# HGRN decays on one Trainium2 core: decayed keys from ScalarE's exponential, queries multiplied on GpSimd

## The reference, cut to what matters

```python
logf = logaddexp(log(lb), log1p(-lb) + log_sigmoid(f_logit))
k = -expm1(logf)
bc = cumsum(logf)                      # within a chunk, per feature
decay = exp(bc[t] - bc[s])             # for s <= t
scores = einsum(q[t], k[s], decay)
o = scores @ v
```

## Time and profile before

| what | value |
|---|---|
| median of 3 runs | 1686.91 us (1686.0 to 1687.82) |
| the profiled execution's own time | 1685.33 us |
| its span in the profile | 1683.5 us |
| mean granted TensorE clock | 0.995 of full |
| layer 0's HGRN levels (first and last score matmul) | 122.05 to 167 us |
| the same in layer 1 | 476.42 to 521 us |

### The profile page before, as it was taken

One profiled execution on the slowest core, in us unless ns is written; L12 is line 12 of the kernel. 1 busy time (PEld: TensorE's weight loads), 2 busy tenths in 40 slices (PEclk: granted clock), 3 DMA queues, 4 the chain that ended last, 5 costly groups with the idle time before them and its releaser, 6 DMA issues.

```text
span 1683.5 us, 30215 instructions
## 1 busy us (share of the span) xinstructions
PE 1622.6 (96%) x11354; PEld 1477.5 (88%) x11354; DVE 1152.7 (68%) x1633; ACT 917.3 (54%) x1576; POOL 444.1 (26%) x184
## 2 busy tenths in 40 slices
PE   8989999999988999999999999999999999999997
PEld 7888799988877899978899989999788999899996
DVE  5687754457787554476784877776758857777767
ACT  5664554446645544465655564455765556554545
POOL 2122122212221222224511122232235311223222
PEclk9999999999999999999999999999999999999999
DMA  9542455646424655546323455665564333466663
GB/s 333 168 126 95 163 202 187 202 161 215 161 72 137 225 190 194 187 160 221 127 95 120 141 186 193 218 202 189 171 209 153 111 101 129 164 212 211 215 197 123
DMA packets 82563, 288.74 MB, mean 172 GB/s; under 512 B 9051, under 2 KB 11908, under 8 KB 81924
## 3 DMA queue, kind: packets, MB, share of 16 engines
q1 hardware_dynamic: 77352, 272.58, 48.6%
q10 hardware_dynamic: 5084, 14.37, 2.6%
HBM read 284.81 MB, written 2.11 MB: 170 GB/s over the span
## 4 chain that ended last, share of the span: by engine, by line
PE 63%; DVE 6%; ACT 2%; issue 2%; DVEq 0%; ACTq 0%
PE bank L727 30%; PE bank L744 26%; PE bank L1301 2%; DVE w_lo L693 1%; PE bank L1282 1%; PE bank L1273 1%; PE bank L1261 1%; PE bank L772 1%; ACT w_hi L689 1%; PE bank L1314 0%; PE bank L781 0%; DVE small L2566 0%; DVE z L2522 0%; PE bank L917 0%; PE bank L925 0%
## 5 line engine op out<-in xcount | busy, mean ns | idle before, releaser
L693 POOL TENSOR_TENSOR w_lo<-raw,w_hi 128x1024 fp32r<-128x1024 f32 x146 | 380.4, 2606 | 1138.7 <-ACT w_hi L689 1138.7
L693 DVE TENSOR_TENSOR w_lo<-raw,w_hi 128x1024 fp32r<-128x1024 f32 x364 | 555.7, 1551 | 146.7 <-ACT w_hi L689 144.8
L689 ACT ACTIVATE w_hi<-raw 128x1024 fp32r<-128x1024 f32 x510 | 518.3, 1051 | 88.7 <-PE bank L744 44.1
L727 PE MATMUL bank<-x_t_hi,w_hi 128*128 128x256 f32 x1984 | 316.9, 282 | 2.3 <-ACT p_t L556 1.6
L727 PE MATMUL bank<-x_t_hi,w_lo 128*128 128x256 f32 x1984 | 307.6, 277 | 0.0
L727 PE MATMUL bank<-x_t_lo,w_hi 128*128 128x256 f32 x1984 | 307.0, 277 | 0.0
L727 PEld LDWEIGHTS bank<-x_t_hi,w_hi 128*128 128x128 f32 x1984 | 270.1, 189 | 14.2 <-issue 5.1
L727 PEld LDWEIGHTS bank<-x_t_hi,w_lo 128*128 128x128 f32 x1984 | 264.5, 188 | 0.0
L727 PEld LDWEIGHTS bank<-x_t_lo,w_hi 128*128 128x128 f32 x1984 | 263.0, 188 | 0.0
L744 PE MATMUL bank<-w_hi,x_t_hi 128*128 128x512 f32 (+3 forms) x448 | 133.6, 381 | 7.3 <-issue 3.4
L744 PE MATMUL bank<-w_hi,x_t_lo 128*128 128x512 f32 (+3 forms) x448 | 131.5, 376 | 1.9 <-DVE x_t_lo L1983 1.9
(11 more groups left out here) (390 smaller groups left out, 2099.7 us busy)
## 6 DMA issues: line engine op xcount, KB each, us to landing
raw<-stream SPq DMA_DIRECT2D x511, 512.0 KB, 4.3
rows<-rows ACTq DMA_DIRECT2D x4, 1024.0 KB, 4.5
gain<-rows ACTq DMA_DIRECT2D x8, 512.0 KB, 3.9
hv_p<-hv_dram ACTq DMA_DIRECT2D x14, 256.0 KB
x<-x_in SPq DMA_DIRECT2D x2, 512.0 KB, 5.1
bias_r<-rev_dram SPq DMA_DIRECT2D x1, 1024.0 KB, 7.2
hv_dram<-hv ACTq DMA_DIRECT2D x2, 512.0 KB, 7.7
y_out<-x SPq DMA_DIRECT2D x2, 512.0 KB, 2.7
```

The costliest lines, as they stand in the source:

```text
L689: self.eng.activation(w_hi[:, i, :], raw[:, i, :], ACT.Copy).then_inc(hi_done.sem, 1)
L693: self.eng.tensor_tensor(w_lo[:, i, :], raw[:, i, :], w_hi[:, i, :].bitcast(F32), ALU.subtract).then_inc((lo_pool if self.part == "pool" e ...
L727: mm = pe.matmul(target, a[:, i, w0 + kt * P:w0 + (kt + 1) * P], b[:, k0 + kt, :], start=kt + k == 0, stop=k == 2 and kt == kts - 1)
```

## The change

The waits on counters are kept in step with the new order; the core of the diff, with the counters' table left out:

```diff
@@ PE, first block
-                pe.wait_ge(*c["decay_in"](at, 1))
+                pe.wait_ge(*c["sig"](at, 2))
...
-                    scores(f"diag{i}", lambda h, t: hk[:, h, t * P:(t + 1) * P], ...
+                    scores(f"diag{i}", lambda h, t: t1[:, h, t * P:(t + 1) * P], ...
@@ ACT, first block
                 def decay_exp(n):
-                    act.wait_ge(*c["decay_in"](at, n + 2))
-                    act.activation(decay_e[:, n % 2, :], decay_e[:, n % 2, :], ACT.Exp).then_inc(c["decay"].sem, 1)
+                    e = decay_e[:, n % 2, :]
+                    if n == 0:
+                        act.wait_ge(*c["key_sums"](at, 1))
+                        act.activation(e[:, 512:].rearrange("p (h s) -> p h s", h=HD), log_f[:, :, P:S], ACT.Exp
+                                       ).then_inc(c["decay"].sem, 1)
+                        for h in range(HD):
+                            ins = act.activation(k_e[:, 0, h * P:(h + 1) * P], hk[:, h, 0:P], ACT.Exp, scale=-1.0,
+                                                 bias=log_f[:, h, P - 1:P])
+                    else:
+                        act.wait_ge(*c["decay_in"](at, n))
+                        act.activation(e[:, 512:], e[:, 512:], ACT.Exp).then_inc(c["decay"].sem, 1)
+                        if n >= 2:
+                            act.wait_ge(*banks.full(at, HG_STEPS[n - 2]))
+                        ins = act.activation(k_e[:, n % 2, :], e[:, 0:512], ACT.Exp)
+                    ins.then_inc(c["k_decay"].sem, 1)
...
-                act.activation(hk[:], hk[:], ACT.Exp, scale=-1.0).then_inc(c["sig"].sem, 1)
+                act.activation(t1[:], hk[:], ACT.Exp, scale=-1.0).then_inc(c["sig"].sem, 1)
+                act.wait_ge(*c["bounds"](at, 1))
+                act.wait_ge(*c["sig"](at, 1))
+                for h in range(HD):
+                    act.activation(log_f[:, h, :], log_f[:, h, :], ACT.Copy, scale=lbc[:, 4 + h:5 + h])
                 projected("kw", nk[:, 1, :])
...
-                act.wait_ge(*c["sig_in"](at, 3))
-                act.activation(t2[:], t2[:], ACT.Ln).then_inc(c["sig"].sem, 1)
+                for h in range(HD):
+                    ins = act.activation(t2[:, h, :], t2[:, h, :], ACT.Ln, scale=lbc[:, 16 + h:17 + h],
+                                         bias=lbc[:, 12 + h:13 + h])
+                ins.then_inc(c["sig"].sem, 1)
@@ DVE, first block
                 def decays(n):
...
+                    if n == 1:
+                        dve.wait_ge(*c["key_sums"](at, 1))
+                    else:
                         dve.wait_ge(*c["k_decay"](at, n - 1))
                         dve.wait_ge(*c["q_decay"](at, n - 1))
...
+                    b, g = (a[:].rearrange("p h s -> p (h s)").rearrange("p (n two s) -> p n two s", two=2, s=s)
+                            for a in (log_f, hk))
+                    ref = b[:, :, 0, s - 1:s].broadcast_to([P, D // (2 * s), s])
+                    dve.tensor_tensor(queries, b[:, :, 1, :], ref, ALU.subtract)
+                    dve.tensor_tensor(keys, ref, g[:, :, 0, :], ALU.subtract).then_inc(c["decay_in"].sem, 1)
-                def decayed_q(n):
...
-                dve.wait_ge(*c["sig"](at, 1))
-                for h in range(HD):
-                    ins = dve.tensor_scalar(t2[:, h, :], t2[:, h, :], omlz[:, h:h + 1], lbz[:, h:h + 1], ALU.mult, ALU.add)
-                ins.then_inc(c["sig_in"].sem, 1)
...
-                dve.wait_ge(*c["sig"](at, 3))
-                for h in range(HD):
-                    ins = dve.scalar_tensor_tensor(log_f[:, h, :], log_f[:, h, :], zero[:, h:h + 1], t2[:, h, :],
-                                                   ALU.mult, ALU.add)
-                step(ins)
                 dve.wait_ge(*banks.full(at, "cmp"))
...
+                dve.wait_ge(*c["sig"](at, 3))
                 for h in range(HD):
                     for t in range(T):
-                        v = log_f[:, h, t * P:(t + 1) * P]
-                        ins = dve.tensor_tensor_scan(v, ones[:], v, 0.0, ALU.mult, ALU.add)
-                step(ins)
+                        v, w = (a[:, h, t * P:(t + 1) * P] for a in (log_f, t2))
+                        ins = dve.tensor_tensor_scan(v, v, w, 0.0, ALU.add, ALU.add)
+                ins.then_inc(c["scanned"].sem, 1)
+                dve.wait_ge(*c["scanned"](at, 1))
...
-                decays(0)
                 decays(1)
                 split.ahead(uid["hg0"])
                 items(7)
-                decayed_q(0)
-                decayed_q(1)
@@ POOL, first block
+                pool.wait_ge(*c["scanned"](at, 1))
+                pool.wait_ge(*c["sig"](at, 2))
+                pool.tensor_tensor(hk[:], hk[:], log_f[:], ALU.add).then_inc(c["key_sums"].sem, 1)
                 split.ahead(uid["hq3"])
-                decayed_k(0)
-                decayed_k(1)
+                decayed_q(0)
+                decayed_q(1)
```

More of the change, by code:

```diff
@@ L2102, in decayed_q @@
-                def decayed_q(n):
-                    dve.wait_ge(*c["decay"](at, n + 1))
-                    if n >= 2:
-                        dve.wait_ge(*banks.full(at, HG_STEPS[n - 2]))
-                    e = decay_e[:, n % 2, :]
-                    if n == 0:
-                        dve.wait_ge(*banks.read(at, "hq3"))
-                        dve.tensor_tensor(q_e[:, 0, :].rearrange("p (h s) -> p h s", h=HD),
-                                          hq[:, :, P:S], e.rearrange("p (h s) -> p h s", h=HD)[:, :, P:S], ALU.mult
-                                          ).then_inc(c["q_decay"].sem, 1)
-                    else:
-                        s = LEVELS[n - 1]
-                        v = e.rearrange("p (n two s) -> p n two s", two=2, s=s)
-                        q = hq[:].rearrange("p h s -> p (h s)").rearrange("p (n two s) -> p n two s", two=2, s=s)
-                        dve.tensor_tensor(q_e[:, n % 2, :].rearrange("p (n s) -> p n s", s=s), q[:, :, 1, :],
-                                          v[:, :, 1, :], ALU.mult).then_inc(c["q_decay"].sem, 1)
+                    s = LEVELS[n - 1]
@@ new lines, in decays @@
+                    keys, queries = (decay_e[:, n % 2, 512 * a:512 * a + 512].rearrange("p (n s) -> p n s", s=s)
+                                     for a in range(2))
+                    b, g = (a[:].rearrange("p h s -> p (h s)").rearrange("p (n two s) -> p n two s", two=2, s=s)
+                            for a in (log_f, hk))
+                    ref = b[:, :, 0, s - 1:s].broadcast_to([P, D // (2 * s), s])
+                    dve.tensor_tensor(queries, b[:, :, 1, :], ref, ALU.subtract)
@@ L2265, in first_block @@
                 level_masked(1)
-                decayed_q(2)
                 if at.index == 0:
@@ L2764, in first_block, with decayed_q @@
                 split.start(at)
-                def decayed_k(n):
+                def decayed_q(n):
                     pool.wait_ge(*c["decay"](at, n + 1))
-                    if n == 0:
-                        pool.wait_ge(*c["decay_in"](at, 1))
                     if n >= 2:
                         pool.wait_ge(*banks.full(at, HG_STEPS[n - 2]))
-                    e = decay_e[:, n % 2, :]
+                    e = decay_e[:, n % 2, 512:]
                     if n == 0:
-                        pool.tensor_tensor(k_e[:, 0, 0:512].rearrange("p (h s) -> p h s", h=HD), hk[:, :, 0:P],
-                                           e.rearrange("p (h s) -> p h s", h=HD)[:, :, 0:P], ALU.mult
-                                           ).then_inc(c["k_decay"].sem, 1)
+                        pool.wait_ge(*banks.read(at, "hq3"))
+                        pool.tensor_tensor(q_e[:, 0, :].rearrange("p (h s) -> p h s", h=HD), hq[:, :, P:S],
+                                           e.rearrange("p (h s) -> p h s", h=HD), ALU.mult
+                                           ).then_inc(c["q_decay"].sem, 1)
@@ L2777, in decayed_k @@
                     else:
                         s = LEVELS[n - 1]
-                        k, v = (a.rearrange("p (n two s) -> p n two s", two=2, s=s)
-                                for a in (hk[:].rearrange("p h s -> p (h s)"), e))
-                        pool.tensor_tensor(k_e[:, n % 2, :].rearrange("p (n s) -> p n s", s=s), k[:, :, 0, :], v[:, :, 0, :],
-                                           ALU.mult).then_inc(c["k_decay"].sem, 1)
+                        q = hq[:].rearrange("p h s -> p (h s)").rearrange("p (n two s) -> p n two s", two=2, s=s)
```

47 lines of the change are left out of this document (13 added, 34 removed).

## The result

| | kernel before | kernel changed |
|---|---|---|
| median, first comparison (22 and 22 runs) | 1687.10 us | 1689.72 us |
| ratio, with its 95% interval | | 1.0017 [1.0009, 1.0025] |
| median, second comparison (23 and 12 runs) | 1688.71 us | 1691.36 us |
| ratio, with its 95% interval | | 1.0022 [1.0012, 1.0032] |
| profiled executions | 1685.33, 1687.43 us | 1692.52, 1689.05 us |

The change costs about 0.2%, some 3 us (1687.10 x 0.0017 = 2.9; 1688.71 x 0.0022 = 3.7). I had forecast 0.5 us less. The first profiled execution of the changed kernel is 2.8 us above its median, so each program was profiled twice. The table by stages shows both; rows are from the first profile unless the text says otherwise.

What follows compares the result with a forecast made beforehand. TensorE, busy 96% of the span, was taken as the bound. Layer 0 at +0.55 and layer 1 at -1.1 gave -0.55, with the clock at 0: 1686.4 us, range 1681.3 to 1690.6.

Steps and rivals of the forecast that it cites:

- one booked at 0: Cross scores in layer 0: the earlier query wins nothing, since the diagonal scores hide it; 0.
- +1.45: First half, each layer: four uncovered ACT copies ahead of the first query's copy make PE, ACT and DVE 1.45 us later.
- +2.75 in all: Item scores at 113.51, each layer: copies, scans held by POOL's split, then POOL's sum make them 2.75 us later.
- rival 2: Behind the item scores of both layers PE's clock falls in the new waits: +5.4, 1691.8 us; chance 0.17.
- Rival 1: Scans not held by POOL, or through before it: item scores +0.55 instead of +2.75, 1682.0 us; chance 0.27.
- -1.65: Cross scores in layer 1: POOL makes the decayed query in time, so PE's wait of 1.65 us goes.
- -2.2: Second half, both layers: DVE, relieved of query products, lets PE's transposes of `no` start 2.2 us earlier.
- Rival 3: Second half: query products on POOL hold DVE's small steps, only 1.2 of 2.2 comes, twice; 1688.4 us; chance 0.10.
- What is late next ... moves along as a whole. 0.: PE's wait for the last mask: its chain over `n_t_hi`, SiLU's tables and a weight split shifts unchanged; 0.
- I count one fall won and one new: 0: PE's clock: layer 0's late fall is spared, a new one comes before the item scores; net 0.
- The one won: Layer 0, from the transposes to `wo4`: a shorter wait spares the clock fall there, which costs 1.7 us.

Runs made afterwards that it cites:

- copies later: The whole change, with the four ACT copies moved behind ACT's copy of the first query; 1686.87 us, 0.9981 of the kernel before.
- sum later: The whole change, with POOL's sum behind DVE's scores of items 10 and 11; 1684.09 us, 0.9974 of the kernel before.
- split and sum later: The whole change, with POOL's split of hq2's last units and its sum behind DVE's item scores; 1683.00 us, 0.9978 of the kernel before.
- the second half: Kernel before plus the change without its first half, POOL's sum waiting for DVE's scores of items 10 and 11; 1685.52 us, 0.9980.
- all three later: The whole change, with copies behind the first query, POOL's split and sum behind the item score, mask unmoved; 1679.78 us, 0.9949 of the kernel before.
- the copies alone: Kernel before plus the four scaled ACT copies at the change's place, written to a tile nobody reads; 1691.14 us, 1.0012.

## Why the prediction was wrong, point by point

I forecast 0.5 us less and measured 2.9 and 3.7 us more. The parts had the right sign, apart from one booked at 0 that won 0.93, and two of their errors cancel. The clock, booked as even, made the difference.

**Copies, "+1.45".** Measured +1.60 in every profile that has them there: four of 0.40 from start to start, no cover. Right in kind, 0.15 short.

**Scans and sum, "+2.75 in all".** Measured +3.31 to +3.35 in four layers. Holding was right, but I had two scans ahead of POOL's split and six behind it. In this profile POOL's split starts at 105.04, 0.15 ahead of the scans, and all eight end behind it. The sum goes so, with times moved by the 0.76 that this profile's fourth item scores are late. The split is 0.18 later than forecast (104.86) and takes 2.41, not 2.35. The scans end 2.49 behind it, not 2.0. From there to the item scores it is 3.67, not 3.80. 0.18 + 0.06 + 0.49 - 0.13 = 0.60, and 2.75 + 0.60 = 3.35. The scans were late because PE ran the projection ahead of the bank of L905 at half clock. This is rival 2's mechanism earlier in the stretch than where I had put it, but it costs the 0.49 and no more: in the second profile the half clock lasted about 6 us instead of 3 and the seventh item scores came no later.

Rival 1 fell: with POOL at work the scans took 3.55 to 4.76, with POOL silent 2.62. Its price was also 0.2 too high by my own terms: 108.85 + 0.17 + 1.22 is 110.24, not 110.05, which makes it 1682.4. The rule of the Trainium skill that I had weighed (SBUF — State Buffer, "Who interferes with whom") is what the trace shows for VectorE, down to a product of 16 columns that waited 2.00 us.

**Cross scores, "-1.65" in layer 1.** The wait of 1.65 vanished, and where no fall stood in the stage it took 9.40 to 9.49 instead of 11.22 (in five of the edited kernels), -1.73 to -1.82. In layer 0, where I had 0, the second profile shows 10.30 instead of 11.23, so -0.93: the wait of 0.77 was there as well, but a clock fall hid it in the profile that I read.

**Transposes of `no`, "-2.2".** 27.08 became 24.87 to 24.97 in three of four layers: -2.2. The wait left is 1.15 to 1.25, not 0.9. Rival 3 fell.

**"What is late next ... moves along as a whole. 0."** At full clock right within 0.2: from the transposes to the last weighing layer 1 took 16.20 before, 16.38 after.

With the shortest time seen for each stage, the kernel before takes 86.49 + 86.48 = 172.97 us in the two layers, the changed one 86.83 + 86.02 = 172.85 (its cross stage in layer 1 taken at 9.49). That is -0.1, near my -0.55, and in part by luck: the first half costs 6.6 us and not 5.5, the cross scores win 2.7 and not 1.65, and the two errors nearly cancel. The actual sums lie above these by 1.45 and 1.11 in the kernel before, and by 7.7 and 3.0 in the changed one. The stages that make up nearly all of this have a stretch at half clock in them. On average over its two profiles the changed kernel pays 2.2 us at the last weighing, 2.1 at the seventh item scores of layer 1 and 0.75 ahead of layer 0's cross scores; the kernel before pays 0.85 at the transposes and 0.3 ahead of the cross scores.

**The step that failed: "I count one fall won and one new: 0"**, with its price of 1.7 for the one won.
- *The one won is worth less.* With the late fall PE comes later to the last mask and waits 1.32; without it, 2.41 (layer 1). Of the 1.7 that the fall costs, 1.1 come back there: 16.73 to 16.81 against 16.20. So here a fall ahead of a wait on another engine's chain is mostly paid by that wait, and so is its absence: without it the wait is 2.41 before and 2.58 in the changed kernel.
- *The new ones are more.* Behind the last wait of 2.58 the clock fell in 10 of the 14 layers that have it (the change twice, copies later, sum later, split and sum later, the second half, and all three later), at 1.0 to 1.6 each; behind the waits of the kernel before and of the one with the copies alone in 0 of 6, but five of these are of 1.31 to 1.33 and one of 2.41. At the seventh item scores of layer 1 it fell in both profiles of the change, +2.7 and +1.5 over the 9.49 of the stage without a fall, and in neither of the kernel before. That this one comes from the change isn't shown: the wait ahead of it is 0.85 in both kernels, and the kernel before with only its last mask moved, the same program up to there, fell at the same place in layer 0. Behind the first wait of 2.36 it fell each time, and that one is inside the +3.35.

That last wait is where the forecast was blind: I had followed it as a length and called it 0, and hadn't asked what the clock does behind it. The chain that sets it isn't on PE. Timeline of DVE in the changed kernel, layer 0:

```profile
167.71 2.52 DVE L693 TENSOR_TENSOR w_lo<-raw,w_hi 128x1024 fp32r<-128x1024 f32 x1 [2.94 <-ACT w_hi L689]
170.16 0.68 DVE L2127 TENSOR_TENSOR am<-bank,consts 128x512 f32<-128x512 f32 x1
```

POOL's split (166.81, 2.35 us) holds this one of DVE to 2.52, where undisturbed ones take 1.22, and the mask stands behind it. Moving the mask in front took the wait away in six of the eight layers where it was tried, with the change and without it; in the other two 2.01 and 0.69 were left.

**Confidence.** By the number the result lies between rival 3 (1688.4) and rival 2 (1691.8); the transposes, 2.2 earlier, rule out rival 3, and the clock falls are rival 2's mechanism, though most of its price stood elsewhere. Rival 2 had 0.17 and one place. It should have had each place where the change leaves a wait in front of dense matmuls, and its price should have been an average over executions.

What stays open: why the clock falls behind the same wait in one execution and not in the next. The counts above are of few executions, and no run here sets the clock by itself. Whether the change makes the falls at the seventh item scores more frequent is open too. The runs' gains are larger than the single profiles show for the last mask (5.5 us by the runs, 1.2 at the matrix of means in its one profile, which had a fall of 2 us in an earlier stage), so profiles place the loss and only the runs size it. The same holds for the copies and the sum: by the ratios each of these two versions is 6 to 8 us below the change, where I expected 2 to 4.

## What to carry to other kernels

Before work goes to another engine, look up what that engine does at this very place and who waits for it: four copies of 0.40 us cost their full length because they stood in front of the instruction that PE waited for, and 1.4 to 2.0 us of half clock on top where nothing else was late. With the copies behind it, and POOL's work moved too, PE lost nothing.

A VectorE instruction with two inputs in SBUF that met one of GpSimd waited here for what was left of it, whatever its own length. So place GpSimd's work where VectorE idles or nobody waits for it.

And price a longer wait of TensorE as the wait plus the slower matmuls behind it; where a wait on another engine's chain follows, time won ahead of it is mostly not won, and half clock ahead of it mostly not lost.

## What was not expected of the hardware

- A VectorE product of 128x16 that takes 0.18 us took 2.18 beside a GpSimd sum of 128x1024 (2.39).
- Eight scans took 3.55 to 4.75 us in one program, and ended at the same distance, 2.49 us, behind a GpSimd instruction each time. That they started up to 1.2 us later against it, behind slower matmuls, made no difference.
- The first half of the change costs 6 to 7 us as it was written, and wins 5.7 once two instructions of GpSimd and four of ScalarE have other places.
- One program, profiled twice, had some of its clock falls in other places, with its first and last waits equal to 0.01 us. The stretch of two layers took 180.59 and 175.86 us. The kernel before had two falls in one profile (174.42) and four in the other (174.08): where a fall lies counts for more than how many there are.
